# Second projection copies turned tiles out first; experts turn tokens behind the up products; norm sums move one stage ahead

## The reference, cut to what matters

```python
for l in range(DEPTH):                      # DEPTH = 2
    mod_lat = (sc_lat @ ada_w[l] + ada_b[l])[:, None, :]
    ...
    a_lat = modulate(rmsnorm(h_lat, norm_mix[l]), sh1, s1)
    a_ctx = modulate(rmsnorm(h_ctx, norm_mix[l]), csh1, cs1)
    if l % 2 == 0:  ... = mixer_ab(a_ctx, ...), mixer_ab(a_lat, ...)   # gated DeltaNet and short conv
    else:           ... = mixer_c(a_lat, a_ctx, rows, cols, ...)       # windowed attention with rotary
    h = h + g1 * y
    f = modulate(rmsnorm(h, norm_ffn[l]), sh2, s2)
    h = h + g2 * hier_moe(f, ...)           # top 2 of 8 experts in the best of 4 groups
return rmsnorm(h_lat, norm_final)

def rmsnorm(x, w):  return x * rsqrt(mean(x * x, -1) + RMS_EPS) * w
# an expert: h = silu(xb @ w1[e]) * (xb @ w3[e]); h @ w2[e]     (D 1024, D_EXPERT 512, 32 experts)
```

## Time and profile before

| what | value |
|---|---|
| median of 3 runs | 3780.85 us (3780.5 to 3790.98) |
| the profiled execution | 3782.25 us, its span 3780.5 us |
| TensorE busy | 3038.9 us, 80% of the span |
| weight loads, VectorE, ScalarE, GpSimd | 1582.7, 1219.4, 673.1, 330.8 us |
| mean granted clock of TensorE | 0.911 |
| `begin` | 0 to 45.48 |
| `norm_mod` of layer 0 | 45.48 to 92.15 |
| `project0` | from 92.15 |
| `experts` of layer 0 | 1422 to 2137, TensorE busy 642.14 |
| `combine` of layer 0 | 2137 to 2192.2 |
| `norm_mod` of layer 1 | 2192.2 to 2231.7 |
| `project1` | 2231.7 to 2505.2, TensorE busy 207.40 |
| `experts` of layer 1, with the last `combine` behind | from 3043.9 |
| idle before the up products | 54.0 us, of it 43.0 for `w<-in_moe_w` |

### The profile page before, as it was taken

The page is one execution under the profiler, slowest core; times in us unless marked ns, Lnnn a source line. Parts: engine busy times, 40 slices in busy tenths (PEclk is TensorE's granted clock), DMA queues, the critical chain, the costliest instruction groups (busy, mean ns, idle before and its releaser), DMA issues. The chain is left out here.

```text
span 3780.5 us, 50933 instructions
## 1 busy us (share of the span) xinstructions
PE 3038.9 (80%) x18238; PEld 1582.7 (42%) x18239; DVE 1219.4 (32%) x2221; ACT 673.1 (18%) x1516; POOL 330.8 (9%) x366
## 2 busy tenths in 40 slices
PE   3999999799976947999998457758889659969992
PEld 1455454588852433333333133335554323323330
DVE  3313413576664351111110342126663421101114
ACT  2212111111130100000000121136661100000002
POOL 0000000211110000000000302111110000000002
PEclk9999999899988968999999768879999779989996
DMA  6511110232334436788988320031101359886874
GB/s 259 159 42 55 35 37 28 79 102 69 97 135 175 172 146 256 319 314 359 389 309 352 139 104 24 29 123 41 62 21 41 145 194 406 354 371 274 364 319 161
DMA packets 152814, 667.46 MB, mean 177 GB/s; under 512 B 26128, under 2 KB 62128, under 8 KB 121936
## 3 DMA queue, kind: packets, MB, share of 16 engines
q1 hardware_dynamic: 123568, 540.05, 37.3%
q0 software_dynamic: 19504, 72.03, 5.0%
q10 hardware_dynamic: 9584, 53.19, 3.4%
HBM read 595.84 MB, written 69.39 MB: 176 GB/s over the span
## 5 line engine op out<-in xcount | busy, mean ns | idle before, releaser
L1795 PE MATMUL bank<-w,xT 128*64 (+1 forms) x3392 | 752.5, 601 | 54.0 <-DMA w<-in_moe_w 43.0
L498 PE MATMUL bank<-aT,w 128*128 128x512 f32 (+1 forms) x1344 | 496.5, 532 | 6.7 <-DVE short L680 5.9
L1795 PEld LDWEIGHTS bank<-w,xT 128*64 128x64 f32 x3392 | 244.4, 139 | 522.7 <-issue 514.0
L1815 PE MATMUL bank<-w,hT 128*64 (+1 forms) x1696 | 381.1, 602 | 37.9 <-issue 37.7
L498 PEld LDWEIGHTS bank<-aT,w 128*128 128x128 f32 x1344 | 263.6, 197 | 235.0 <-issue 219.9
L1887 DVE TENSOR_TENSOR h<-h,bank 128x512 f32<-128x512 f32 x53 | 36.4, 687 | 785.0 <-PE bank L1795 785.0
L1815 PEld LDWEIGHTS bank<-w,hT 128*64 128x64 f32 x1696 | 124.8, 138 | 292.6 <-issue 290.4
L2081 PE MATMUL bank<-at_w_in,aT 128*128 128x512 f32 x416 | 191.5, 622 | 2.9 <-PEq L116 2.9
L2269 PE MATMUL bank<-eye,probs 128*128 128x128 f32 x640 | 98.8, 286 | 45.7 <-ACT probsT L2333 45.5
L1771 PE MATMUL bank<-eye,x 128*128 128x128 f32 x440 | 65.5, 295 | 82.6 <-DMA x<-moe_x,idx_block 58.1
L2081 PEld LDWEIGHTS bank<-at_w_in,aT 128*128 128x128 f32 x416 | 83.2, 203 | 105.6 <-issue 105.6
(11 more groups left out here) (333 smaller groups left out, 3918.7 us busy)
## 6 DMA issues: line engine op xcount, KB each, us to landing
w<-in_moe_w SPq DMA_DIRECT2D x180, 2048.0 KB, 14.2
ada_w<-in_ada_w SPq DMA_DIRECT2D x48, 1024.0 KB, 7.9
moe_y<-y ACTq DMA_DIRECT2D x53, 512.0 KB
w<-in_moe_w ACTq DMA_DIRECT2D x12, 2048.0 KB, 27.5
w<-in_ab_w_in SPq DMA_DIRECT2D x28, 512.0 KB, 3.9
moe_y<-zero POOLq DMA_DIRECT2D x1, 8192.0 KB, 27.6
moe_x<-a SPq DMA_DIRECT2D x13, 512.0 KB, 2.6
at_w_in<-in_at_w_in SPq DMA_DIRECT2D x3, 2048.0 KB
```

The costliest lines, as they stand in the source:

```text
L498: mm = pe.matmul(k.bank[3 * s + n][:, 0:width], w[j][:, c, :], aT[:, c, at:at + width], start=(c == 0), stop=(c == KC - 1))
L1795: mm = pe.matmul(k.bank[UP[half]][u * UNIT:(u + 1) * UNIT, :], xT[:, c, u * UNIT:(u + 1) * UNIT], w13[:, r if u else ds(buf[0], 1), half, ...
L1815: mm = pe.matmul(k.bank[Y[half]][u * UNIT:(u + 1) * UNIT, :], hT[:, c, u * UNIT:(u + 1) * UNIT], w2[:, r if u else ds(buf[0], 1), at:at + ...
```

## The change

`First` loads `w_ab` and the first weight tile of `project0` while `norm_mod` of layer 0 runs. The squares, mean, root and reciprocal of the two norms that precede a projection are made at the end of the stage that has `H` ready: in `begin` once `H` has landed (ahead of `finish` and `store`), in `combine` of layer 0 by ScalarE behind the adds. In `experts` SyncE waits for the first gather before it loads further weights; on TensorE `up(0)` comes ahead of `turn_x(1)`, and in the body `turn_x(j + 1)` comes behind `up(j)`. In `project1` ScalarE takes the turned groups of tile t - 1 before it copies `z` of tile t; for that it first waits that the stores of that buffer are done.

```diff
+class First:
+    def __init__(self, k):
+        self.src = k.dram["ab_w_in"][0].rearrange("(j p) n -> p j n", p=P)
+        self.w, self.wab = k.sb("w0", [P, KC, P]), k.sb("w_ab", [P, KC, 4 * NH])
+        self.w_in, self.wab_in = k.sem("w_in0"), k.sem("w_ab_in")
+    def load(self, sp):
+        sp.dma_start(self.wab[:], self.src[:, :, 4 * W0:4 * W0 + 4 * NH]).then_inc(self.wab_in, 16)
+        sp.dma_start(self.w[:], self.src[:, :, 0:P]).then_inc(self.w_in, 16)
...
 def begin(k):            # scalar
         mod.consts(act)
+        act.wait_ge(h_in, 64)
+        for n, t in enumerate(ours):
+            if n:
+                act.wait_ge(act_sums, n)
+            nc.scalar.activation(sq[:, 0, :], H[:, t, :], ACT.Square, accum_out=rstd[:, t:t + 1]).then_inc(act_sums, 1)
+        act.wait_ge(mean_ready, 1)
+        nc.scalar.activation(rstd[:], rstd[:], ACT.Sqrt).then_inc(root_ready, 1)
         mod.store(act)
...                       # vector
+        dve.wait_ge(h_in, 64)
+        for n, t in enumerate(theirs):
...
+        dve.wait_ge(dve_sums, len(theirs))
+        dve.wait_ge(act_sums, len(ours))
+        nc.vector.tensor_scalar(rstd[:], rstd[:], 1.0 / D, EPS, ALU.mult, ALU.add).then_inc(mean_ready, 1)
+        dve.wait_ge(root_ready, 1)
+        nc.vector.reciprocal(rstd[:], rstd[:])
         mod.finish(dve, 0)
...
 def norm_mod(...):       # scalar and vector: the squares, mean, root and reciprocal are gone
...
 def project0(k, aT, ahead):   # sync
-        sp.dma_start(wab[:], dr["ab_w_in"][0, :, ALPHA:SC].rearrange("(j p) n -> p j n", p=P)).then_inc(wab_in, 16)
-        for j in range(PARTS):
+        for j in range(1, PARTS):
...
 def experts(...):        # sync
+        sp.wait_ge(x_in, 16)
         for m in range(ring.AHEAD, NE):
...                       # tensor
         turn_x(0)
+        up(0, *owners(0))
         turn_x(1)
-        up(0, *owners(0))
         def body(j):
             of_block = owners(j)
-            turn_x(j + 1)
             turn_h(j - 1)
             up(j, *of_block)
+            turn_x(j + 1)
             down(j - 1)
...
 def combine(...):        # scalar, layer 0 only
+            for n in range(T):
+                act.wait_ge(added[n % 2], primed(n // 2 + 1))
+                if n:
+                    act.wait_ge(sum_ready, primed(n))
+                nc.scalar.activation(sq[:, 0, :], H[:, first + n, :], ACT.Square, accum_out=r[:, n:n + 1]).then_inc(sum_ready, 1)
+            act.wait_ge(mean_ready, primed(1))
+            nc.scalar.activation(r[:], r[:], ACT.Sqrt).then_inc(root_ready, 1)
...                       # vector, layer 0 only
+            dve.wait_ge(sum_ready, primed(T))
+            nc.vector.tensor_scalar(r[:], r[:], 1.0 / D, EPS, ALU.mult, ALU.add).then_inc(mean_ready, 1)
+            dve.wait_ge(root_ready, primed(1))
+            nc.vector.reciprocal(r[:], r[:])
...
 def project1(...):       # scalar; take_turned(t) copies the groups of tile t from banks 6 and 7
-        for t in range(NT + 1):
+        for t in range(NT):
+            s = t % 2
+            if t:
+                act.wait_ge(stored[1 - s], primed(stores(t - 1)))
+                take_turned(t - 1)
             act.wait_ge(z_ready, primed(t + 1))
...                       # z copies, wait for the rope, keys copy, as before
-            if t > 0:
-                u = t - 1
-                for g in ((2,) if u < CT else (0, 1, 2)):
...
+        take_turned(NT - 1)
```

More of the change, by code:

```diff
@@ L235, in begin @@
     mod = Modulation(k, [(0, 0)], KC, 0)
+    sq, rstd, H = k.sb("squares", [P, 2, D]), k.rstd, k.H
+    act_sums, dve_sums = k.sem("act_sums", 0), k.sem("dve_sums", 0)
+    mean_ready, root_ready = k.sem("mean_ready", 0), k.sem("root_ready", 0)
+    ours, theirs = [t for t in range(NT) if t % 3 != 2], [t for t in range(NT) if t % 3 == 2]
     block = k.block()
@@ L309, in _ @@
             mod.consts(act)
[L310 to L315, removed]
         for i in range(NT // 2):
@@ L328, in _ @@
     def _(dve):
[L329 to L340, removed]
         dve.wait_ge(rows_in, primed(16 * 2 * len(vs)))
@@ L369, in _, with project0 @@
                 mod.products(pe, EVERY * i, EVERY * i + EVERY if i < NT // 2 - 1 else KC * len(parts))
-def project0(k, aT):
+def project0(k, aT, ahead):
     nc, dr = k.nc, k.dram
@@ L381, in project0 @@
     COLS = (0, W0, 2 * W0, QC, SC + W0, SC + 2 * W0, SC)
-    w = [k.sb(f"w{j}", [P, KC, P]) for j in range(PARTS)]
-    wab = k.sb("w_ab", [P, KC, 4 * NH])
+    w = [ahead.w] + [k.sb(f"w{j}", [P, KC, P]) for j in range(1, PARTS)]
+    wab, wab_in = ahead.wab, ahead.wab_in
     cq = k.sb("conv_qkv", [P, 3, 3 * NH])
@@ L392, in project0 @@
     r = k.sb("inv_norm", [P, 2, 512])
-    w_in = [k.sem(f"w_in{j}") for j in range(PARTS)]
+    w_in = [ahead.w_in] + [k.sem(f"w_in{j}") for j in range(1, PARTS)]
     w_used = [k.sem(f"w_used{j}") for j in range(PARTS)]
-    wab_in = k.sem("w_ab_in")
     consts_in, ones_set, pads_set = k.sem("consts_in"), k.sem("ones_set"), k.sem("pads_set")
@@ L2106, in _ @@
     def _(act):
-        for t in range(NT + 1):
[L2108 to L2124, removed]
-                    act.wait_ge(turned, primed(rounds(t - 1)))
-                nc.scalar.copy(kd[s][:], keys.unsqueeze(2).to_broadcast([P, ATT_KV, 2, HD])).then_inc(kd_ready, 1)
-            if t > 0:
-                u = t - 1
-                for g in ((2,) if u < CT else (0, 1, 2)):
-                    r = rounds(u) + (g if u >= CT else 0)
-                    act.wait_ge(turned, primed(r + 1))
-                    nc.scalar.copy(out[u % 2][:, 4 * g:4 * g + 4, :].rearrange("p c n -> p (c n)"),
-                                   k.bank[6 + r % 2][:]).then_inc(taken, 1)
@@ L2446, in build @@
         k.logits = k.sb("logits", [P, NT, GROUPS + NE])
+        k.rstd = k.sb("rstd", [P, NT])
         with k.scope():
@@ L2454, in build @@
                 aT = k.sb("aT", [P, KC, TOK])
+                first = First(k)
                 with k.scope():
-                    norm_mod(k, 0, 0, 0, aT, parts=[(0, 1)])
+                    norm_mod(k, 0, 0, 0, aT, early=first, parts=[(0, 1)])
                 with k.scope():
-                    project0(k, aT)
+                    project0(k, aT, first)
             with k.scope():
```

41 lines of the change are left out of this document (34 added, 7 removed).

## The result

The changed kernel takes 3735.09 us in the median of four runs (3731.38 to 3737.16), the kernel before 3780.68 in four beside it (3777.27 to 3790.98). The ratio is 0.9879, 95% interval 0.9857 to 0.9901: 45.7 us less (37 to 54), where 49.9 were forecast. (Here and in the experiments, a difference in us that stands behind a ratio is that ratio times the median of before; the plain difference of the two medians is up to 3 us off it.) The profiled execution took 3731.38 us with a span of 3729.6, so 50.9 less than the profiled one of before.

A forecast was written before the change was run, and what follows sets the result against it. The prediction took TensorE, busy for 80% of the span, to bound the kernel, so its standstills count. Terms of -60.2, -28.0, +34.4, +2.3 and +1.6 sum to -49.9, giving 3731 us from 3780.85; range 3685 to 3752.

The forecast's parts named there:

- Project1, -60.2: Project1: ScalarE's earlier takes free the last transposes, cutting the period from 32.45 to 22.3 us; 60.2 us less.
- the seventh stall: Project1: the stop behind the last projection stays, since nothing covers the rope of tile 9; 0.8 us added.
- Rival 2: Project1 gives only half its gain because keys or stores bind: 3761 us, chance 0.1.
- Experts, loop, +34.4: Experts' body: the new order leaves more sequencer work uncovered, 0.6 us for each of 47 blocks plus 6: +34.4 us.
- the stalled blocks: Experts' loop: in four blocks where up waits long for weights or code, turn_x is no longer hidden: +6 us.
- the hold: Experts' body: before turn_x's 8 transposes enter TensorE's full queue, 8 matmuls must start: 1.74 us.
- the 1.07: Experts' body: forecast idle time before down, in us, with turn_x ahead of it; +0.5 a block.
- Rival 1: Experts' loop: the sequencer has room, so idle before down vanishes (3680 us) or stays as is (3697); chance 0.25.
- Experts, start, -28.0: Start of both MoEs: gather 0 lands 7.0 us earlier and the second turn leaves the path; 28.0 us less.
- First norm, +2.3: Sums moved into begin cost +10.5, norm_mod gains 4.3 and project0 3.9: +2.3 us in all.
- Second norm, +1.6: Combine gains 3.0 us of square, root and reciprocal; norm_mod saves 1.4: +1.6 us.
- Rival 3: Experts: longer stops in each body lower the clock, half of 3.4 us in all 51 bodies: 3818 us, chance 0.05.

The follow-up runs named there:

- e5: The kernel before with only the new order of the experts' body (turn_h, up, turn_x, down), old start kept: 3814.18 us, ratio 1.009.
- e4: The changed kernel with the five table reads for down(j-1) moved ahead of turn_x(j+1): 3692.01 us, ratio 0.977 to the kernel before.
- e2: The kernel before with only the experts' new start (SyncE waits for gather 0, up(0) ahead of turn_x(1)): 3782.17 us, ratio 1.0001.
- e3: The changed kernel with the experts' loop body put back to its old order: 3727.63 us, ratio 0.9856 to the kernel before.
- e6: The kernel before with only the norm sums moved into begin and combine, without the early loads: 3787.65 us, ratio 1.0017.
- e9: The kernel before with only the early loads of w_ab and w0 in norm_mod: 3776.60 us, ratio 0.9988.
- e10: The changed kernel with down's table reads ahead of turn_x, and begin's finish and store before and between the sums: 3689.46 us, ratio 0.9767 to the kernel before.

## Why the prediction was right, step by step

The forecast of 3731 missed by 4 us, and no step of it failed that decides its sign or size. Two things in it were wrong and did no harm here: the experts' two edits were priced as if their terms add, and the loop's term came out right partly because misses cancel. By its terms:

- **Project1, -60.2: -59.3.** Period 22.43 for 22.3, the seventh stall kept at 9.27. Rival 2 (keys or stores bind) does not show: the only stop in the six covered turns is 0.29 us.
- **Experts, loop, +34.4: +33.6** (e5). The three parts: before down +0.34 for +0.5, before up +0.37 for +0.3, top -0.20 for -0.2; the 51 bodies make that 26. The 7 left are not the 6 laid to the stalled blocks. The trace of e5 has no such loss: the three longest steps from one down to the next within a layer are 36.4, 44.4 and 38.3 us before and 36.3, 44.5 and 37.6 in e5. What the prediction put at nothing is the 0.10 between up and turn_x, and turn_h's transposes, which take 0.10 more a body (busy 34.8 us before, 39.9 in the changed kernel). Without the long waits a step from down to down grew by 0.64 in the mean. So the term is right in mechanism, and its close agreement in size is partly luck. The step that decided, a sequencer held at 18 matmuls, is shown twice: by the 10 + 8 in the changed kernel, and by e4, where the reads moved ahead of the transposes took away 43 us. From the branch at 1486.6 to the first read at 1488.3 pass 1.7 us, where the prediction had 1.74 for the hold. The prediction worked with the profile's own idle time. By that measure the base of 0.6 was right (0.59), and the 1.07 is too high: 0.93 in the mean. Rival 1 is out.
- **Experts, start, -28.0: -26.5, but only together with the new body.** The prediction took the terms for additive. e2 and e3 show that they aren't: the start moves turn_x(1) behind up(0), so gather 2 goes out behind up(0) and no longer ahead of it, and only the new body, which asks for it behind up(1) and no longer ahead of it, can bear that. The prediction had "A gather keeps its 23 us" for the loop and didn't ask the same of the start by itself. That gather 1 and the weights disturb each other stood only in its bounds (-22 to -30). In e2 gather 1 took 11.5 us for 3.4 and gather 2 10.9 for 3.6; in the changed kernel, where they take 11 too, no turn_x waits for them.
- **First norm, +2.3: +4.5.** Begin +11.1 for +10.5 and project0 -4.1 for -3.9 are right; in begin each square now waits for the one before, so that they come 1.18 us apart for 1.04 before. The mis-sized term is norm_mod's -4.3, which measured -2.5: the earlier trace rows were read as if the rows had the DMA engines to themselves for 7.5 us. e6 puts their landing at 9.0.
- **Second norm, +1.6: 0.** Behind combine's last add come 3.0 us of square, root and reciprocal, as worked out. But in the kernel before the barrier's release came 3.3 us behind that add (2188.92 to 2192.20), in the changed kernel 4.2. In both kernels GpSimd drains for 1.7 us behind its last add before it joins the barrier. Before, everything waited for that; now it runs beside ScalarE's square and root, so that of their 3.0 us about 1 is left to pay (the stage took 1.1 more).

The timeline of combine's end after, for the last point:

```profile
2191.51 2.34 POOL L1964 TENSOR_TENSOR H<-H,y 128x1024 f32<-128x1024 f32 x1 [4.88 <-DVE y L2005]
...
2196.58 0.22 DVE L2025 RECIPROCAL rstd<-rstd 128x10 f32<-128x10 f32 x1 [1.35 <-ACT rstd L1990]
2198.01 0.32 SPq L307 DMA_DIRECT2D scale_rows<-mods  x1
```

Rival 3 (the clock falls in each body) shows nowhere: stops before down of 0.6 to 1.5 us by the profile's rows, 0.93 in the mean, left the mean clock of the experts' stage of layer 0 at 0.98, before 0.97. Two rows of windows, before and after:

```profile
1422.20:2137.30 715.10, 642.14 (x3032) 238.88 (x3032) 75.49 (x113) 51.41 (x86) 33.59 (x58) 0.97 0.77 306
```

```profile
1422.70:2142.00 719.30, 648.25 (x3032) 239.91 (x3032) 78.06 (x113) 51.35 (x86) 33.46 (x58) 0.98 0.76 304
```

So the change is one large gain in project1, and three reorderings elsewhere that almost cancel: experts +7.1, norms and early loads +4.5.

## What to carry to other kernels

Where a stop is put down to "issue", look at the engine's sequencer: how many matmuls it still had in front of it when the branch ran, and what it reads behind that point. Try register reads ahead of short instructions rather than behind them: here the reads then ran under long matmuls already queued, which was worth 43 us for one moved line. And before two edits of a pipeline are priced one by one, ask for each whether the buffer's next fill is still issued in time without the other; a prologue and a loop body that take turns with one buffer have one price together.

## What the runs showed of the hardware

- In the bodies read here the sequencer of TensorE ran 18 matmuls with their 18 weight loads ahead, the pair under way counted, and short transposes fill those places like long matmuls: 18 left at the branch, then 8 transposes put in and 10 left at the first read.
- Five reads from the table took 3.8 us of the sequencer (1488.3 to 1492.1 in the changed kernel's body), 0.75 each at that pace, of which the read itself is 0.30.
- A gather of 512 KB landed in 3.5 us with nearly empty queues and in 11 beside weights (in e2 3.48 for the first, 11.53 and 10.87 for the next two).
- A stage without an edit, the delta scan, scattered by 6.4 us over thirteen executions. A term below that size is better read from its own stage than from the whole, and there from its own wait: project0, too, took 583.3 and 588.4 us in two kernels (e9 and e10) that are alike in it.
